# Weight buffers at the end of the partition, everything behind them 49152 bytes lower

## The reference

```python
# first_block, per layer
u = h @ w_in[l]                       # 1024 x 2564; then attention, pooling, retention, convolution
x = x + g1 * (mix @ w_out[l])         # 1024 x 1024
f = (silu(h @ ffn_w1[l]) * (h @ ffn_w3[l])) @ ffn_w2[l]   # 1024 x 2816 twice, 2816 x 1024
# second_block, per layer
h = x @ w_in[i]                       # 1024 x 2116; then top-k attention and spatial gating
mix = concat([a_out, b_out]) @ w_o[i] # 1024 x 1024
gate, up = split(x @ w_ffn_in[i])     # 1024 x 5632
ffn = (silu(gate) * up) @ w_ffn_out[i]            # 2816 x 1024
ple = (p[i] @ w_ple[i]) * sigmoid(x @ w_ple_gate[i])
```

## The kernel before

| Tensor | address before | mod 128 / 64 | address in the change | mod 128 / 64 |
|---|---|---|---|---|
| x | 16512 | 0 / 0 | 16512 | 0 / 0 |
| h_hi, h_lo | 32896, 49280 | 0 / 0 | the same | 0 / 0 |
| raw (2 x 8192) | 65664 | 0 / 0 | 180192 | 96 / 32 |
| w_hi (2 x 8192) | 82048 | 0 / 0 | 196576 | 96 / 32 |
| w_lo (2 x 8192) | 98432 | 0 / 0 | 212960 | 96 / 32 |
| eye, ones, ..., eye_r, pick_r | 114816 to 118912 | 0 / 0 | 49152 lower | 0 / 0 |
| mid: f_hi, m_sq | 128672 | 32 / 32 | 79520 | 32 / 32 |
| f_lo | 173728 | 32 / 32 | 124576 | 32 / 32 |
| n_mask | 182720 | 64 / 0 | 133568 | 64 / 0 |
| e_hi, e_lo | 205248, 209344 | 64 / 0 | 49152 lower | 64 / 0 |
| end of the usable partition | 229344 | | 229344 | |

## Time and profile before

### The profile page before, as it was taken

One profiled execution on the slowest core, in us unless ns is written; L12 is line 12 of the kernel. 1 busy time (PEld: TensorE's weight loads), 2 busy tenths in 40 slices (PEclk: granted clock), 3 DMA queues, 4 the chain that ended last, 5 costly groups with the idle time before them and its releaser, 6 DMA issues.

```text
span 2610.1 us, 30256 instructions
## 1 busy us (share of the span) xinstructions
PE 2489.1 (95%) x11670; PEld 1993.8 (76%) x11670; DVE 1070.5 (41%) x1718; ACT 884.0 (34%) x1153; POOL 1075.8 (41%) x373
## 2 busy tenths in 40 slices
PE   7799999999999999999999999999989998999997
PEld 4576788878777788888787678888769776888875
DVE  5798520069477640000496440000247746000014
ACT  4225422222425422222443542222233354222222
POOL 0334255544234055553253435554424533555442
PEclk8899999999899999999999999999999999999998
DMA  7513432267322433323321213222332211222231
GB/s 276 178 55 119 149 97 93 90 206 223 99 81 81 161 97 97 96 78 99 99 79 59 65 65 97 96 96 83 99 91 81 73 49 65 97 96 96 88 93 61
DMA packets 297044, 267.89 MB, mean 103 GB/s; under 512 B 20104, under 2 KB 273784, under 8 KB 296696
## 3 DMA queue, kind: packets, MB, share of 16 engines
q1 hardware_dynamic: 296952, 266.63, 32.5%
HBM read 264.51 MB, written 2.10 MB: 102 GB/s over the span
## 4 chain that ended last, share of the span: by engine, by line
PE 80%; DVE 9%; issue 6%; ACT 2%; POOL 2%; DMA 1%; SPq 0%; DVEq 0%; ACTq 0%; POOLq 0%
PE bank L2361 25%; PE bank L2363 24%; PE bank L2362 24%; DVE m_cv L1828 2%; POOL w_lo L1351 1%; PE bank L2896 1%; DVE g_acc L1588 1%; ACT w_hi L817 1%; PE bank L2814 1%; PE bank L2929 1%; PE bank L2608 1%; DVE small L1714 0%; PE bank L2863 0%; DVE a_acc L1588 0%; DVE n_qi L2165 0%
## 5 line engine op out<-in xcount | busy, mean ns | idle before, releaser
L1351 POOL TENSOR_TENSOR w_lo<-raw,w_hi 128x2048 fp32r<-128x2048 f32 (+1 forms) x201 | 849.3, 4225 | 1179.1 <-ACT w_hi L817 1152.3
L2361 PE MATMUL bank<-h_hi,w_lo 128*128 128x512 f32 (+1 forms) x2192 | 871.3, 398 | 50.3 <-DVE h_lo L1695 22.7
L2362 PE MATMUL bank<-h_lo,w_hi 128*128 128x512 f32 (+1 forms) x2192 | 860.2, 392 | 0.0
L2363 PE MATMUL bank<-h_hi,w_hi 128*128 128x512 f32 (+1 forms) x2192 | 859.9, 392 | 0.0
L2361 PEld LDWEIGHTS bank<-h_hi,w_lo 128*128 128x128 f32 (+1 forms) x2192 | 415.6, 190 | 155.0 <-issue 61.9
L817 ACT ACTIVATE w_hi<-raw 128x2048 fp32r<-128x2048 f32 (+1 forms) x216 | 378.3, 1751 | 444.4 <-PE bank L2363 417.0
L2362 PEld LDWEIGHTS bank<-h_lo,w_hi 128*128 128x128 f32 (+1 forms) x2192 | 415.6, 190 | 89.0 <-issue 3.0
L2363 PEld LDWEIGHTS bank<-h_hi,w_hi 128*128 128x128 f32 (+1 forms) x2192 | 414.9, 189 | 89.2 <-issue 0.4
L1738 DVE TENSOR_TENSOR f_full<-f_act,bank 128x512 f32<-128x512 f32 x88 | 60.5, 687 | 840.0 <-PE bank L2363 840.0
L2361 PE MATMUL bank<-f_hi,w_lo 128*128 128x512 f32 x704 | 280.4, 398 | 2.4 <-POOL w_lo L1351 2.4
L2363 PE MATMUL bank<-f_hi,w_hi 128*128 128x512 f32 x704 | 278.8, 396 | 0.0
(11 more groups left out here) (356 smaller groups left out, 2315.7 us busy)
## 6 DMA issues: line engine op xcount, KB each, us to landing
raw<-in_ffn_w SPq DMA_DIRECT2D x44, 1024.0 KB
raw<-in_w_ffn_in SPq DMA_DIRECT2D x44, 1024.0 KB
raw<-in_w_in SPq DMA_DIRECT2D x34, 1024.0 KB
raw<-in_ffn_w SPq DMA_DIRECT2D x32, 704.0 KB
raw<-in_w_ffn_out SPq DMA_DIRECT2D x32, 704.0 KB
b_raw<-in_ada_w SPq DMA_DIRECT2D x16, 1024.0 KB, 8.0
a_raw<-in_ada_w SPq DMA_DIRECT2D x32, 512.0 KB, 4.7
z_a<-in_ada_w SPq DMA_DIRECT2D x4, 2048.0 KB, 14.3
```

What stands on the lines that cost most here:

```text
L1351: pool.tensor_tensor(b.w_lo[p][:, 0:n], b.raw[p][:, 0:n], b.w_hi[p][:, 0:n].bitcast(F32), ALU.subtract)\
L2361: pe.matmul(out, wlo, xhi, start=start, stop=False)
L2362: pe.matmul(out, whi, xlo, start=False, stop=False)
L2363: return pe.matmul(out, whi, xhi, start=False, stop=stop)
```

## The change

`raw`, `w_hi` and `w_lo` get addresses counted back from the end of the partition, 6 x 8192 bytes in all. What stood behind them moves 49152 bytes lower, since the space they took is free, and the assertion and the two tensors `rows` and `rows2` that stood at the partition's end are now counted from `end`. No instruction, no wait, no order and no shape changes on any engine; each instruction names the same tensors.

```diff
+        end = (nc.sbuf_usable_end & ~31) - 6 * 8192
-        b.raw = [place(f"raw{i}", [P, 2048], F32) for i in range(2)]
-        b.w_hi = [place(f"w_hi{i}", [P, 2048], F32R) for i in range(2)]
-        b.w_lo = [place(f"w_lo{i}", [P, 2048], F32R) for i in range(2)]
+        b.raw = [place(f"raw{i}", [P, 2048], F32, at=end + 8192 * i) for i in range(2)]
+        b.w_hi = [place(f"w_hi{i}", [P, 2048], F32R, at=end + 8192 * (2 + i)) for i in range(2)]
+        b.w_lo = [place(f"w_lo{i}", [P, 2048], F32R, at=end + 8192 * (4 + i)) for i in range(2)]
...
-                assert self.at <= nc.sbuf_usable_end, (self.tag, name, self.at - nc.sbuf_usable_end)
+                assert self.at <= end, (self.tag, name, self.at - end)
...
-        b.rows = place("rows", [74, P], F32, at=(nc.sbuf_usable_end & ~31) - 8 * P)
-        b.rows2 = place("rows2", [2 * TAPS, P], F32, at=(nc.sbuf_usable_end & ~31) - 4 * P)
+        b.rows = place("rows", [74, P], F32, at=end - 8 * P)
+        b.rows2 = place("rows2", [2 * TAPS, P], F32, at=end - 4 * P)
```

## The result

| | before | changed |
|---|---|---|
| device time, median of 4 runs each | 2613.66 us (2610.55 to 2615.7) | 2658.93 us (2653.44 to 2661.0) |
| ratio to before, 95% interval | | 1.0173 [1.0158, 1.0189] |
| span of the profiled execution | 2610.1 us | 2656.0 us |
| mean granted TensorE clock | 0.976 | 0.975 |

The forecast was 2620.5 us with a range up to 2655. The change costs 45.3 us by the medians and 45.9 us by the spans. It doesn't come from the clock, which is the same.

The account below looks back on a forecast made before the run. It took TensorE's matmul streams as the bound; all terms were 0 except +5.9 us for weights as moving operand, added to the median 2614.6 us for 2620.5 us, with an 8-in-10 range of 2607 to 2655.

Parts of the forecast that it names:

- What bounds the kernel: TensorE, busy 95% of the span and holding 80% of the last chain, so the cost per streamed matmul counts.
- weights as stationary operand: 8784 matmuls that load moved weights: taken as 0 because loads are hidden, upper bound 6.5 ns each, 57.1 us.
- Rows 5: Profile rows before the change: weight loads of 68 columns gave the same pitch as 128, three taking 0.68 us.
- The reading of the four pitches: Moving operand's own start sets cost: 6.5 ns more at 32 off a multiple of 64, 2.3 at 64 off 128.
- Weights as moving operand: Matmuls with w moving, 256 columns: 6.5 ns more on each of 912 on the chain, +5.9 us.
- ScalarE, GpSimd, copies at 0: Engine work on weights and weight copies: any slowdown hidden behind waits or spare DMA time, so 0.
- Rival 2, first form: Distance between moving and stationary operands costs in h, f streams: +39.7 us, 2654 us; 19% for both forms, mostly this.
- Rival 1: No dependence on addresses anywhere; f's extra has another cause and time stays at 2614.6 us; 18%.
- rival 2's second form: A misplaced stationary weight costs by itself: +63.0 us, 2678 us; minor part of 19%.
- rival 3: Moving weights away from h ends memory-region conflicts in h matmuls: up to 77 us faster, 2538 us; 18%, strong form 12%.
- Rival 3's weak form: Moving operands above 128 KB cost: f_hi gains 9.2 us, weights lose 5.9, giving 2611 us; 6%.

Follow-up runs that it names:

- phase_all: Kernel before with freq and window merged into one tensor and the region of the e operands begun 224 bytes later; 2603.39 us, ratio 0.996.
- f_phase: Kernel before with freq and window merged into one tensor, so everything behind them lies 32 bytes lower; 2605.9 us, ratio 0.9959.
- low_off96: Kernel before with raw, w_hi and w_lo 96 bytes higher in their old place, everything behind them 128 higher; 2653.95 us, ratio 1.0153.
- low_off64: Kernel before with 64 bytes added ahead of raw and 64 more behind w_lo; 2649.78 us in one run.
- low_off128: Kernel before with everything from raw on 128 bytes higher; 2646.86 us, ratio 1.0115.
- f_aligned: Kernel before with all that starts at mid (f, e and n_mask among it) 96 bytes higher; 2619.54 us, ratio 1.0025.
- h_w_off32: Kernel before with h_hi, h_lo, raw, w_hi and w_lo all at remainder 32 on 128, the rest at old remainders; 2616.11 us, ratio 1.001.
- raw_only_off96: Changed kernel with w_hi and w_lo at multiples of 128, in phase with h, and raw alone at remainder 96 on 128; 2618.7 us, ratio 1.001.
- end_aligned: Changed kernel with its end rounded down to a multiple of 128, weights still at the partition's end; 2616.51 us, ratio 1.0007.
- lo_only_off96: Kernel before with w_lo alone 96 bytes higher and everything behind it 128 higher; 2648.08 us, ratio 1.012.

## Why the prediction was wrong

| (moving minus stationary) mod 256 | pitch in cycles of 2.4 GHz, 512 columns moving, and which |
|---|---|
| 0 | 544 (h before; f and e in phase_all) |
| 32 | 560 (f before; e in f_phase) |
| 64 | 549 (e before), 554 (f in low_off96) |
| 96 | 560 (f in low_off64), 559 (e in low_off96) |
| 128 | 559 (h in low_off128, f in f_aligned and h_w_off32), 557 (e in low_off64) |
| 160 | 562 (h after) |
| 192 | 560 (f after, h in low_off64) |
| 224 | 560 (e after) |

- **What bounds the kernel** was right: TensorE's streams, at full clock.
- **The step that failed is "weights as stationary operand", taken as 0** of a bound of 57.1 us. It measured 6576 x 7.5 ns = 49.3 us, and its own reason was wrong: a weight load that nearly halves "without a trace in the pitch is hidden". That row was taken in phase. Out of phase the load's length does show. In the changed kernel these two starts of the same kind are 27 pitches apart, and a third of the loads between them have 68 columns:

```profile
1299.15 0.39 PE L2362 MATMUL bank<-h_hi,w_lo 128*68 128x512 f32 x1
...
1305.43 0.39 PE L2362 MATMUL bank<-h_hi,w_lo 128*68 128x512 f32 x1
```

They take 6.28 us, 232.6 ns each, and the pitches between two 68-column loads are 231.0 ns in the mean; where all loads have 128 columns it is 234.2. Rows 5 tested whether the load is longer than the matmul, not whether the pitch depends on it at other addresses.
- **The reading of the four pitches was wrong in kind.** 0, 32 and 64 are the differences of h, f and e from w as well as their own remainders, since before w stood at remainder 0 (modulo 256 at 128, as h does). I saw that ("no row separates") and gave the simpler reading 45%. f_aligned and h_w_off32 show it to be false.
- **Weights as moving operand, +5.9 us**, measured 0: the pitch stays 120.4 ns. By low_off64 these units depend on addresses too, but not at the value reached here.
- **ScalarE, GpSimd, copies at 0**: right, by the rows above. The Trainium skill's rule ("DMA: Bandwidth & Descriptors", section "How a descriptor splits into AXI transactions") on transfers off a multiple of 256 bytes, an estimate of 8% more per copy and up to 3 us in the forecast, is not borne out by the queue that carries the copies. The pages of the profile before (`raw` 128 off) and after (224 off):

```profile
q1 hardware_dynamic: 296952, 266.63, 32.5%
```
```profile
q1 hardware_dynamic: 296952, 266.63, 32.2%
```

32.5% of 2610.1 us are 848 us and 32.2% of 2656.0 us are 855, 0.8% more for all packets together, of which `raw`'s carry about three quarters of the bytes. TensorE's waits for w_lo fell from 8.3 to 7.5 us. raw_only_off96 can't decide this, since its `raw` is 96 off.
- **Rival 2, first form**, is what happened. Its 2654 us are 5 under the median: it took 6.5 ns for 7.5 (6.6 us), counted 5.9 us for w moving that aren't there, and let f fall by 8.9 us, which would need a period of 128; f went from 32 to 192 without effect. It got only 19%, since I let the hidden loads speak against it, and beside them the Trainium skill ("SBUF — State Buffer", section "Who interferes with whom"), which gives TensorE separate read ports for moving data and weight loads. The measurements decide otherwise: the matmul takes 5 to 18 cycles more than 544 by nothing but the relative start of the two.
- **Rival 1** (no dependence), **rival 2's second form** (the weights' own place) and **rival 3** (the region) are refuted by low_off96, h_w_off32 and end_aligned. Rival 3's weak form, f gaining by lying below 128 KB, fell with the changed kernel itself: f 233.3 ns at 79520.
- **The range** ended at 2655, at rival 2's central value without its spread. An end that reaches a rival has to take in the rival's own error.

What stays open is the mechanism behind the 256 bytes. The runs show a dependence on the difference of starts, that 256 is a period of it and 128 isn't, that a load of 68 columns costs less out of phase than one of 128, and that one buffer out of phase slows its neighbours. That the moving read and the weight load disturb each other fits all of this, but no run separates it from another cause.

## What to carry to other kernels

A layout change can cost time though no instruction changes. In a stream of 512-column float32r matmuls, keep the starts of moving and stationary operands equal modulo 256, and look at the pitch of each kind of stream after every move of a tensor. If two kinds of stream in one trace differ by 2 to 3% at the same shape and clock, suspect their addresses first; here merging two small tensors gained 0.4%. A row that shows a resource as hidden under good conditions says nothing on how it behaves when the conditions go.

## What was unexpected of the hardware

- The difference of two start addresses sets the pitch of split matmuls: 544 cycles at 0, 549 to 562 at every other multiple of 32.
- In the changed kernel h's pitches repeat over seven matmuls: 231, 234, 235, 233, 232, 237, 238 ns, 1640 in all. In phase they lie at 226 or 227 ns.
- With 256 columns moving and activations stationary the best place is another: 116.7 ns (low_off64), 118.2 (lo_only_off96), 119.1 (low_off128), 120.4 at 0 and in the change.
- Where VectorE and GpSimd meet, one of them stands still, and which one can differ between layouts: GpSimd's operation takes 5.44 us and VectorE's ten 6.71 us, or 1.45 and 14.47 us with four more GpSimd operations beside the ten. GpSimd's can be held over six whole VectorE operations, not only over the one that runs when it begins.
